# Delta rule of two stacked blocks: second head pair's joins run as one block after the first scan, with first-level copies on ScalarE, later query products and earlier key loads

## The reference, cut to what matters

```python
def _gated_delta_chunked(q, k, v, g, beta):
    ...
    g = jnp.cumsum(g, axis=-1)
    decay = jnp.where(tri, jnp.exp(jnp.where(tri, diff, 0.0)), 0.0)
    kb = k * beta[..., None]
    a_mat = jnp.where(strict, jnp.einsum('bhncd,bhnsd->bhncs', kb, k) * decay, 0.0) + jnp.eye(C, dtype=jnp.float32)
    rhs = jnp.concatenate([v * beta[..., None], kb * jnp.exp(g)[..., None]], axis=-1)
    sol = lax.linalg.triangular_solve(a_mat, rhs, left_side=True, lower=True, unit_diagonal=True)
    u, w = sol[..., :Dv], sol[..., Dv:]
    intra = jnp.einsum('bhncd,bhnsd->bhncs', q, k) * decay

    def step(S, inp):
        q_c, k_c, u_c, w_c, g_c, a_c = inp
        v_new = u_c - jnp.einsum('bhcd,bhde->bhce', w_c, S)
        o = jnp.einsum('bhcd,bhde->bhce', q_c * jnp.exp(g_c)[..., None], S) + jnp.einsum('bhcs,bhse->bhce', a_c, v_new)
        g_last = g_c[..., -1]
        S = S * jnp.exp(g_last)[..., None, None] + jnp.einsum(
            'bhcd,bhce->bhde', k_c * jnp.exp(g_last[..., None] - g_c)[..., None], v_new)
        return S, o
```

## Time and profile before

| | us |
|---|---|
| median of 3 runs (2582.14 to 2588.27) | 2583.44 |
| profiled execution, device time | 2581.91 |
| its span in the trace | 2580.1 |
| PE busy | 2451.8 |
| DVE busy | 1675.4 |
| ACT busy | 1127.4 |
| POOL busy | 917.7 |

### The profile page before, as it was taken

How to read it: one execution, slowest core, us unless ns; L and a number is a source line. 1 busy time by engine, 2 the same in 40 slices (tenths; PEclk the granted TensorE clock), 3 DMA queues, 4 the chain that set the end, 5 groups by cost and what they waited for, 6 DMA issues and landing times.

```text
span 2580.1 us, 33373 instructions
## 1 busy us (share of the span) xinstructions
PE 2451.8 (95%) x12995; PEld 1977.1 (77%) x12995; DVE 1675.4 (65%) x2284; ACT 1127.4 (44%) x1867; POOL 917.7 (36%) x627
## 2 busy tenths in 40 slices
PE   8999998987879999999999999899999999999997
PEld 6788876666768888888888787666687888888885
DVE  6565665766566865665687738677567665566876
ACT  5544445644444433332344534566444332333443
POOL 2333241576015565555200045311346555551000
PEclk9999998998789999999999999899999999999999
DMA  4222406343135233323764233100251323329443
GB/s 163 86 91 103 162 33 228 103 158 108 61 122 173 65 107 107 113 93 104 267 217 137 69 128 103 41 9 1 94 151 53 115 94 103 119 87 329 125 135 104
DMA packets 136284, 300.64 MB, mean 117 GB/s; under 512 B 30272, under 2 KB 30656, under 8 KB 136000
## 3 DMA queue, kind: packets, MB, share of 16 engines
q1 hardware_dynamic: 136128, 298.52, 34.4%
HBM read 220.80 MB, written 77.66 MB: 116 GB/s over the span
## 4 chain that ended last, share of the span: by engine, by line
PE 74%; DVE 11%; ACT 5%; POOL 5%; issue 2%; DMA 1%; SPq 1%; DVEq 0%; ACTq 0%; POOLq 0%
PE ps L380 20%; PE ps L381 20%; PE ps L382 20%; ACT t L396 4%; PE ps L1003 2%; PE ps L987 2%; PE ps L1023 2%; POOL t L2776 1%; DVE t L669 1%; POOL t L1479 1%; POOL t L2784 1%; POOL t L1476 1%; DVE t L730 1%; DVE t L1137 1%; ACT t L1086 1%
## 5 line engine op out<-in xcount | busy, mean ns | idle before, releaser
L396 ACT ACTIVATE t<-t 128x512 fp32r<-128x512 f32 (+5 forms) x1176 | 771.5, 696 | 1111.5 <-PE ps L382 660.2
L380 PE MATMUL ps<-t 128*128 128x512 f32 (+1 forms) x2778 | 1088.9, 392 | 27.4 <-DVE t L649 8.7
L381 PE MATMUL ps<-t 128*128 128x512 f32 (+1 forms) x2778 | 1081.2, 389 | 0.0
L382 PE MATMUL ps<-t 128*128 128x512 f32 (+1 forms) x2778 | 1081.1, 389 | 0.0
L380 PEld LDWEIGHTS ps<-t 128*128 128x128 f32 x2778 | 523.9, 189 | 143.8 <-issue 17.7
L381 PEld LDWEIGHTS ps<-t 128*128 128x128 f32 x2778 | 524.0, 189 | 109.2 <-issue 2.6
L382 PEld LDWEIGHTS ps<-t 128*128 128x128 f32 x2778 | 523.7, 189 | 108.5
L2776 POOL TENSOR_TENSOR t<-t 128x512 fp32r<-128x512 f32 x280 | 417.9, 1497 | 355.1 <-ACT t L396 355.1
L483 POOL TENSOR_TENSOR t<-t 128x1024 fp32r<-128x1024 f32 x80 | 199.9, 2502 | 577.6 <-ACT t L396 577.6
L2504 DVE TENSOR_TENSOR t<-ps,t 128x512 f32<-128x512 f32 x200 | 136.8, 687 | 201.8 <-PE ps L382 201.7
L396 ACT ACTIVATE t<-ps 128x512 f32<-128x512 f32 (+4 forms) x314 | 159.8, 538 | 133.3 <-PE ps L1627 43.0
(11 more groups left out here) (199 smaller groups left out, 2349.1 us busy)
## 6 DMA issues: line engine op xcount, KB each, us to landing
t<-in_wts_dram SPq DMA_DIRECT2D x172, 512.0 KB, 3.5
t<-g_d SPq DMA_DIRECT2D x148, 256.0 KB, 2.7
g_d<-t SPq DMA_DIRECT2D x144, 256.0 KB, 2.1
t<-in_wts_dram SPq DMA_DIRECT2D x110, 256.0 KB, 5.0
t<-pj SPq DMA_DIRECT2D x39, 512.0 KB, 5.6
pj<-t SPq DMA_DIRECT2D x32, 512.0 KB, 2.7
t<-in_xT_dram SPq DMA_DIRECT2D x32, 256.0 KB, 6.7
x_d<-t SPq DMA_DIRECT2D x32, 256.0 KB, 4.2
```

The lines of the kernel that those rows point to most:

```text
L380: e.matmul(out, ah, bh, start=start, stop=False, skip_group_check=goes_on)
L381: e.matmul(out, ah, bl, start=False, stop=False, skip_group_check=goes_on)
L382: return e.matmul(out, al, bh, start=False, stop=stop, skip_group_check=goes_on)
L396: return e.activation(out, in_, fn, scale=scale)
```

## The change

The second pair's joins no longer lie between the steps of scan 0: scan 0 runs alone with six banks, then `queries(2)`, `queries(3)`, `first_x` and the joins of pair 1 follow as one block, then scan 1. In pair 0's block, `first_x` comes ahead of `keys(2)`, `differences(3)` comes ahead of everything on DVE, `scaled_row` of head 3 goes from POOL to DVE, and `keys(3)` and the two `backward` come after the first three units. The first level's X copies go from DVE to ACT (`l_x1_a`). Of the eight decayed keys one goes to DVE and two to POOL; the beta scaling of the odd heads' forward chains goes from ACT to DVE. POOL's third attention gate comes ahead of head 2's rows (33 for 35), and its zeroing after the fourth gate. SP loads the keys of heads 1 and 0 ahead of the gather, head 3's after blocks in, head 2's after blocks out. The scatter's two halves get a semaphore each, so a head waits only for its own.

```diff
-    NA_GATES = [14, 22, 35, 38]
+    NA_GATES = [14, 22, 33, 38]
...
-                    scaled_row(e, w, 2, d)
+                    scaled_row(e, w, 2, d, False)
...
+            if i == 38:
+                for d in range(2):
+                    zeros(e, w, 2, d)
...
-    q_first = [N_.raws[1][0], N_.raws[1][1], X[:, 6, :], X[:, 7, :]]
+    q_first = [N_.raws[1][0], N_.raws[1][1], D_.q[:], X[:, 7, :]]
...
+    kd_of = lambda h, d: d_kd_v if (h, d) == (1, 1) else d_kd_p if (h, d) in ((2, 1), (3, 1)) else d_kd
+    tb_of = lambda h, d: d_tb_v if d or h % 2 else d_tb
+    scat_of = lambda h: (scat[1 if h == 3 else 0], h // 2)
+
+    def decayed_keys(e, w, h, d):
+        w.wait_ge(l_p, (h, d, 1))
+        w.wait_ge(kt_load[h % 3], h)
+        return e.tensor_tensor(v8(D_.R[h][d][:]), v8(X[:, kt_at[h], :]), bcl(ed[:, :, hd_of(h, d)]), MUL)
...
     def pe_delta(e, w):
...
-        keys(2)
         for a in range(4):
             first_x(0, a, slots_d)
-        between = {0: lambda: backward(2), 2: lambda: keys(3), 4: lambda: backward(3), 6: lambda: queries(2),
-                   8: lambda: queries(3)}
+        keys(2)
         for i, u in enumerate(LEVELS):
             level(0, u, slots_d)
-            if i in between:
-                between[i]()
...
-        scan(0, banks_0, second)
...
+            if i == 0:
+                keys(3)
+                backward(2)
+            if i == 2:
+                backward(3)
+        banks_s.until[:] = [slots_d.until[1 + i // 2] for i in range(6)]
+        scan(0, banks_s, lambda i: None)
+        slots_d.until[1:] = [banks_s.until[2 * i] + banks_s.until[2 * i + 1] for i in range(3)]
+        queries(2)
+        queries(3)
+        for a in range(4):
+            first_x(1, a, slots_d)
+        for u in LEVELS:
+            level(1, u, slots_d)
+        banks_s.until[:] = [slots_d.until[1 + i // 2] for i in range(6)]
+        slot_f.until[:] = slots_d.until[0:1]
+        scan(1, banks_s, lambda i: finish(i // 2 - 3) if i in (6, 8) else None)
...
     def dve_delta(e, w):
...
-            if what == "XY" or d == 1:
+            if what == "F" and d == 1:
                 w.wait_ge(l_x, key)
...
-            if what == "F" and d == 1:
+            if what == "F" and (d or h % 2):
...
+        differences(e, w, 3)
         keys(2)
...
             level(0, u, slots_d)
...
+            if i == 0:
+                for d in range(2):
+                    scaled_row(e, w, 3, d, False)
+                keys(3)
+        decayed_keys(e, w, 1, 1).then_inc(*d_kd_v.up((1, 1)))
+        scan(0, banks_s, lambda i: None)
+        queries(2)
+        queries(3)
+        for u in LEVELS:
+            level(1, u, slots_d)
...
     def act_delta(e, w):
...
+            if what == "XY":
+                key = (h, d, l)
+                w.wait_ge(l_x, key)
+                for o in BELOW[l]:
+                    m = act(e, v8(D_.X[h][d])[lower(l, o), :, upper(l, o)],
+                            v8(slots_d[("x",) + key][lower(l, o), 0:8 * SIDE[l]]), ACT.Copy)
+                m.then_inc(*l_x1_a.up(key))
-            if what == "P" and l == 1:
+            if what == "P" and l == 1 and kd_of(h, d) is d_kd:
...
-            if what == "F" and d == 0:
+            if what == "F" and d == 0 and h % 2 == 0:
...
     def pool_delta(e, w):
         for d in range(2):
-            scaled_row(e, w, 3, d)
+            zeros(e, w, 3, d)
         for _ in blocks(e, w, 1):
             pass
+        for h in (2, 3):
+            decayed_keys(e, w, h, 1).then_inc(*d_kd_p.up((h, 1)))
...
     def sp_delta(e, w):
         def kt(h):
-            w.wait_ge(*((na_park[3], 3) if h == 0 else (d_qk, h + 1) if h < 3 else (d_kd, (0, 1))))
+            w.wait_ge(*((na_park[3], 3), (NA.value, (11, 1)), (d_qk, 3), (d_kd, (0, 1)))[h])
...
         q_again(0)
+        kt(1)
+        kt(0)
         sp_gather(e, w, 1)
         sp_blocks_in(e, w, 1)
-        kt(0)
-        kt(1)
+        q_again(1)
+        kt(3)
+        sp_blocks_out(e, w, 1)
         kt(2)
-        kt(3)
-        q_again(1)
-        sp_blocks_out(e, w, 1)
         q_again(2)
         q_again(3)
```

More of the change, by code:

```diff
@@ L506, in build @@
     x_in1, w0_in = na_load[0] + na_load[1], tab_load[0]
-    wg_in = dma("wg")
+    wg_in = row_store[1]
     kind = {}
@@ L1442, in differences, with zeros, scaled_row @@
             m.then_inc(*d_diff.up((h, d)))
-    def scaled_row(e, w, h, d):
+    def zeros(e, w, h, d):
+        w.wait_ge(*((d_db_v if h == 3 else d_db), (h, d)))
+        e.memset(D_.Y[h][d][:], 0.0).then_inc(*d_zero.up((h, d)))
+    def scaled_row(e, w, h, d, zero=True):
         w.wait_ge(d_exp, (h, d))
         w.wait_ge(brow_load[row_sig(h, d)], h)
-        e.tensor_tensor(D_.R[h][d][:], D_.D[h][d][:], brow[h][d][:], MUL).then_inc(*d_db.up((h, d)))
-        w.wait_ge(d_db, (h, d))
-        e.memset(D_.Y[h][d][:], 0.0).then_inc(*d_zero.up((h, d)))
+        e.tensor_tensor(D_.R[h][d][:], D_.D[h][d][:], brow[h][d][:], MUL).then_inc(
+            *(d_db_v if h == 3 else d_db).up((h, d)))
+        if zero:
+            zeros(e, w, h, d)
     def pool_delta_early(e, w, i):
@@ L1592, in level @@
             if what == "XY" or d == 1:
-                p = place(r, ("x",) + key, [(l_x1, key)])
-                w.wait_ge(*((scat, b) if l == 0 else (l_y1, (h, d, 0))))
+                p = place(r, ("x",) + key, [(lx1_of(l), key)])
+                w.wait_ge(*(scat_of(h) if l == 0 else (l_y1, (h, d, 0))))
                 for c, o in corners:
@@ L1653, in pe_delta @@
                             NA.tring.until[2] + [(NA.out, len(na_pairs) // 4 - 1)]]
-        keys(2)
         for a in range(4):
             first_x(0, a, slots_d)
-        between = {0: lambda: backward(2), 2: lambda: keys(3), 4: lambda: backward(3), 6: lambda: queries(2),
-                   8: lambda: queries(3)}
+        keys(2)
         for i, u in enumerate(LEVELS):
             level(0, u, slots_d)
-            if i in between:
-                between[i]()
-        slots_l.until[:] = slots_d.until[0:2]
-        banks_0.until[:] = [slots_d.until[2 + i // 2] for i in range(4)]
-        def second(i):
-            for u in JOINS.get(i, []):
-                if u[0] == "T":
-                    first_x(1, u[1], slots_l)
-                else:
-                    level(1, u, slots_l)
-        scan(0, banks_0, second)
-        banks_1.until[:] = [slots_l.until[1]] * 2 + banks_0.until
-        slot_f.until[:] = slots_l.until[0:1]
-        scan(1, banks_1, lambda i: finish(i // 2 - 3) if i in (6, 8) else None)
+            if i == 0:
[15 more added lines that the diff above has]
+        scan(1, banks_s, lambda i: finish(i // 2 - 3) if i in (6, 8) else None)
         finish(2)
@@ L1720, in level @@
                 m.then_inc(*l_y1.up(key))
-            if what == "F" and d == 1:
-                w.wait_ge(l_x1, key)
-                e.tensor_tensor(v8(X_), v8(X_), bcl(beta[:, :, hd_of(h, d)]), MUL).then_inc(*d_tb_v.up((h, d)))
+            if what == "F" and (d or h % 2):
+                w.wait_ge(l_x1 if d else l_y1, key)
+                T = v8(T_of(h, d)[:])
+                e.tensor_tensor(T, T, bcl(beta[:, :, hd_of(h, d)]), MUL).then_inc(*d_tb_v.up((h, d)))
         def scan(b, r, between):
@@ L1782, in dve_delta @@
         w.wait_ge(na_park[1], 1)
+        differences(e, w, 3)
         keys(2)
-        between = {0: lambda: differences(e, w, 3), 4: lambda: keys(3), 6: lambda: queries(2), 8: lambda: queries(3)}
         for i, u in enumerate(LEVELS):
             level(0, u, slots_d)
-            if i in between:
-                between[i]()
-        def second(i):
-            for u in JOINS.get(i, []):
-                if u[0] != "T":
-                    level(1, u, slots_l)
-        scan(0, banks_0, second)
+            if i == 0:
[8 more added lines that the diff above has]
+            level(1, u, slots_d)
         ends_of = {0: [(0, 0)], 2: [(0, 1), (1, 0)], 4: [(0, 2), (1, 1)], 6: [(1, 2)], 8: [(0, 3)], 10: [(1, 3)]}
-        scan(1, banks_1, lambda i: [finish(h, part) for h, part in ends_of.get(i, [])])
+        scan(1, banks_s, lambda i: [finish(h, part) for h, part in ends_of.get(i, [])])
         for part in range(4):
@@ L1859, in act_delta @@
             first_x(0, a, slots_d)
+        decays(e, w, 3)
         backward(2)
-        decays(e, w, 3)
-        backward(3)
-        for u in LEVELS:
-            level(0, u)
-        def second(i):
-            for u in JOINS.get(i - 1, []):
-                if u[0] == "T":
-                    first_x(1, u[1], slots_l)
-                else:
-                    level(1, u)
-        scan(0, banks_0, second)
-        second(16)
+        for i, u in enumerate(LEVELS):
+            level(0, u)
+            if i == 2:
+                backward(3)
+        scan(0, banks_s, lambda i: None)
+        for a in range(4):
+            first_x(1, a, slots_d)
+        for u in LEVELS:
+            level(1, u)
```

(2 more changed lines are left out.)

44 lines of the change are left out of this document (23 added, 21 removed).

## The result

| | before | after |
|---|---|---|
| median of the runs, us | 2583.4 | 2564.7 (2564.2 to 2565.0) |
| profiled execution, us (span) | 2581.91 (2580.1) | 2564.93 (2563.1) |
| ratio after / before | | 0.9925 [0.9913, 0.9938] |

The change makes the kernel 18.7 us faster. The forecast was 31.5 us faster (2552), and the result lies above the high end of its range, 2564.

What follows compares the result with a forecast made beforehand. Two chains (joins and scans; gather, inverse and scatter) and PE's queue taking the later bound the stretch. Scan 1's step 1 moves from 702.97 to 671.5, a gain of 31.5 us, so 2550.4 profiled, 2552 median; range 2545 to 2564.

Steps and rivals of the forecast that it cites:

- differences(3): First on DVE in pair 0's preparation: its second half starts at 568.2, takes half of 4.50 us, ends at 570.5.
- The row's landing: Ahead of differences(3)'s second half: a row issued at 561.69 needs 6.5 us to land, so that half waits until 568.2.
- First block: Pair 0's joins ahead of scan 0: lower clock in the first third only, step 1 at 603.9 against 619.11.
- Scan 0: Seven steps at 4.98 us, bound by the chain through S, end at 638.8.
- Second block: Pair 1's joins between scan 0 and scan 1: begin at 646.6 and end at 667.0, PE's units at the upper clock.
- rival 2: Pair 1's block of joins runs at the lower clock: 9 us more, gain 22.5, 2561 us; chance 0.13.
- The scatter: Behind POOL's inverse, ahead of pair 1's transposes: halves ready at 641.8 and 643.9, the first about when the queries end, 642.9.
- rival 1: Loads ahead of the gather start POOL at 598.4 or later; the block waits for the scatter until about 647: 2556; chance 0.17.
- the lower bound: Start of POOL's inverse: the copy of head 3's transpose alone limits the gather, giving 591.2; the forecast took 594.6.
- the 4.26 us row: SP's queue before the change: the gather's third issue stood 4.26 us behind loads, until 586.0; it speaks for the late scatter.
- ACT's wait for keys: Scan 0's start: keys of heads 0 and 1 are loaded by then, so ACT's 9.33 us idle should disappear.
- kt(2): Load of head 2's keys, issued after the scatter, could hold ACT: landing at 697 gives +8, 2592 us; slower, chance 0.03.

Runs made afterwards that it cites:

- Experiments 1 and 2: Changed kernel with POOL's gates of channels 2 and 3 cut to 64 columns: 2557.8 us; with channel 3's gate and head 2's scaled rows on DVE: 2559.3 us.
- experiment 8: Changed kernel with 128x128 products ahead of each P and X unit: three in both blocks, 2576.9 us; one, in the second block alone, 2563.6 us.
- experiment 7: Changed kernel with queries(2) and (3) inside scan 0: 2564.0 us; in halves, with POOL's products also taken from beside the differences: 2558.5 us.

## Why the prediction was right and wrong

From NA's last pair, the forecast's terms (555.83 taken off its times) and what after shows (559.64 taken off):

| step | forecast | after | off by, in this step |
|---|---|---|---|
| differences(3) ends | 14.7 | 21.5 | +6.8 |
| keys(3) ends | 23.4 | 29.4 | -0.8 |
| scan 0, step 1 | 48.1 | 56.6 | +2.5 |
| scan 0 ends | 83.0 | 91.3 | -0.2 |
| second block's joins begin | 90.8 | 99.0 | -0.1 |
| last scaling | 111.2 | 122.7 | +3.3 |
| step 1 of scan 1 | 115.7 | 126.7 | -0.5 |

The sum is 11.0 us in the stage. Another 3.8 us came before it, and 0.4 less behind it: 14.4, against 14.5 for the 2564.93 of the profiled execution less the 2550.4 forecast for it. (Two of the forecast's sums are 0.2 us off: 583.2 adds up to 583.0, and the middle of 591.2 and 598.4 is 594.8. Neither matters.)

**differences(3), the step that failed.** "Half of 4.50 us follows: 570.5" took a length from a place where POOL was idle for most of it and carried it to a place where POOL had three products to do. Each of DVE's instructions that met one took up to 2.45 us instead of 0.34. `differences(2)`, which the change doesn't move, paid 2.1 us because the third gate (channel 2's) went from step 35 to step 33; the forecast put nothing for that gate beside the differences, and nothing for the rows and the fourth gate beside `differences(3)`. Experiments 1 and 2 show it by taking the products away. The forecast had the rule in its hands and used it on the inverse alone, where it was right: 40.8 us forecast, 40.8 measured (601.51 to 642.32). What was missed is its size here. The Trainium skill (SBUF — State Buffer, SBUF: two separate sides) says that the shared pair is an exclusive lock for a whole instruction, and that a DVE instruction with two SBUF inputs contends only with a GpSimd one that reads SBUF. The traces agree on both: the longest difference lasts 2.446 us beside products of 2.40, and the zeroings cost nothing.

**The row's landing** was named as what gates `differences(3)`. Without POOL it might have been the gate, but in after nothing waited for it.

**First block, +2.5.** The forecast put the lower clock in the first third only; it was 0.50 throughout. By experiment 8 a full PE alone would not have changed that: the joins' own products didn't bring the clock back.

**Scan 0** was right in length: 34.7 us against 34.9. The reason given for it, "bound by the chain through S", holds only in part: PE is busy 14.07 of 15 us, so more work on PE lengthens a step too. It cost nothing here, but it made me expect 3 to 5 us from experiment 7, which gave 0.6.

**Second block, +3.3.** That is rival 2, the block at the lower clock. It came true, at a third of its price of 9 us, as PE's 25.5 us and DVE's work overlap. From the last scaling to step 1 it took 4.1 us where 2.5 were counted, as the step's groups of products ran at 0.50 too (2.08 and 1.91 us, against 1.17 and 1.06 in the next step); that used up most of the 2.0 us of allowance.

**The scatter** (rival 1) did come late, and PE came later still. The forecast had its first half at 86.0 us behind the pair, rival 1 at 91.2; the last of its four issues stands at 648.29 and took 2.1 to 2.4 us to land, which makes 91. PE asked for it at 94.9, so nothing waited. The reason was not the rival's: the copy of head 3's transpose came 6.1 us late and set the inverse's start, as the lower bound had it (593.1 and 8.0 make 601.1, measured 601.51). So the inverse ended 82.7 us behind the pair, no sooner than the 82.5 before. The store and its landing took 4.4 us where 2.6 were counted. Whether the loads caused the 4.26 us row, on which that rival rested, stays open; in after no single issue took more than 1.39.

**Right besides:** ACT's wait for keys is gone and is worth 7.9 us; the block is the main gain, 14.3 us (together more than the 20.4 us of the stage, so the two are not separate gains); kt(2) held up nobody.

## What to carry to other kernels

Before a step on VectorE with two SBUF operands is moved, look at what GpSimd does at its new place, not at how long it took at the old one; each GpSimd product beside it cost here up to 2.1 us, nearly its own 2.4, and putting a product on VectorE itself (1.2 us here) can be cheaper than that. Price a block of small matmuls at the lower clock from the start, even where PE is never idle: the joins here ran at 0.50 in windows that were full. Compare two traces from the last event that the change can't touch, since what lies ahead of it moved by 2.3 us between three executions of one kernel here, and by 5.0 among those of all the changed ones.

## What the runs showed of the hardware

- A VectorE instruction with two SBUF inputs lasted 2.45 us instead of 0.34 beside a GpSimd product of 2.40, and where GpSimd's products followed each other without a gap, one VectorE instruction was hit for each (experiments 1 and 2). Beside GpSimd's zeroings, and for VectorE's instructions with a PSUM input, no such length was seen. Where VectorE's series was already running, GpSimd's product was the one to take longer: the first scaled row, begun at 569.65 among differences of 0.34 us, took 3.16 us, the second 2.40, against 2.37 and 2.35 before.
- Products of 32 and 64 columns filled PE's row (5.00 of 5 us) and still ran at the 1.2 GHz level; with one product of 128x128 ahead of each unit PE stayed at the 2.4 GHz level, and its products of 64 columns took 221 ns instead of 314.
- The same code was granted 0.95 of the clock in one execution and 0.83 in another in the stretch of 460 to 480 us.
